# Gate and up rounds 3 to 10 as 2x2x2 block products in seven products

## The reference

```python
def swiglu(h, w_gate, w_up, w_down):
    return (jax.nn.silu(h @ w_gate) * (h @ w_up)) @ w_down
...
    h = h + swiglu(rms_norm(h, ffn_norm[i]), ffn_w_gate[i], ffn_w_up[i], ffn_w_down[i])
```

## Time and profile before

| what | value |
|---|---|
| median of 3 runs | 1115.61 us (1115.36 to 1115.8) |
| time of the profiled execution | 1115.62 us |
| its span | 1113.8 us |
| TensorE (PE) busy | 1102.3 us, 99% |
| VectorE (DVE) busy | 569.3 us, 51% |
| ScalarE (ACT) busy | 333.5 us, 30% |

### The profile page before, as it was taken

One profiled execution on the slowest core, in us unless ns is written; L12 is line 12 of the kernel. 1 busy time (PEld: TensorE's weight loads), 2 busy tenths in 40 slices (PEclk: granted clock), 3 DMA queues, 4 the chain that ended last, 5 costly groups with the idle time before them and its releaser, 6 DMA issues.

```text
span 1113.8 us, 13079 instructions
## 1 busy us (share of the span) xinstructions
PE 1102.3 (99%) x5056; PEld 916.9 (82%) x5056; DVE 569.3 (51%) x777; ACT 333.5 (30%) x407; POOL 40.1 (4%) x22
## 2 busy tenths in 40 slices
PE   8999999999999999999999999999999999999997
PEld 7888888888888888888888888888888888888886
DVE  6667766565454544333447545766454545433332
ACT  6667762322122121121232211323121221212221
POOL 0232230000000000000000000000000000000000
PEclk9999999999999999999999999999999999999999
DMA  7211221322322222222212233222323222222211
GB/s 275 95 66 48 75 74 40 114 113 76 113 82 107 80 108 104 75 104 104 104 75 78 111 114 107 83 79 109 114 75 113 81 108 81 107 104 98 76 63 75
DMA packets 16956, 106.08 MB, mean 95 GB/s; under 512 B 1888, under 2 KB 2144, under 8 KB 6432
## 3 DMA queue, kind: packets, MB, share of 16 engines
q1 hardware_dynamic: 16848, 105.43, 26.2%
q0 software_dynamic: 80, 0.26, 0.1%
HBM read 103.59 MB, written 2.10 MB: 95 GB/s over the span
## 4 chain that ended last, share of the span: by engine, by line
PE 97%; DMA 1%; DVE 1%; ACT 1%; SPq 0%; issue 0%; DVEq 0%; ACTq 0%
PE bank L406 32%; PE bank L408 32%; PE bank L407 32%; PE bank L560 1%; PE bank L546 1%; DMA head<-head_in 1%; PE bank L439 0%; DVE head L1405 0%; PE bank L548 0%; PE bank L445 0%; PE bank L453 0%; ACT a_hi L727 0%; ACT w_hi L713 0%; DVE mid_lo L1032 0%; ACT L849 0%
## 5 line engine op out<-in xcount | busy, mean ns | idle before, releaser
L406 PE MATMUL bank<-a_hi,w_hi 128*128 128x512 f32 x1000 | 391.9, 392 | 2.3 <-DVE a_lo L1078 2.0
L408 PE MATMUL bank<-a_hi,w_lo 128*128 128x512 f32 x1000 | 389.3, 389 | 0.0
L407 PE MATMUL bank<-a_lo,w_hi 128*128 128x512 f32 x1000 | 389.2, 389 | 0.0
L713 ACT ACTIVATE w_hi<-raw 128x2048 fp32r<-128x2048 f32 (+1 forms) x98 | 180.1, 1838 | 651.5 <-PE bank L408 651.3
L989 DVE TENSOR_TENSOR w_lo<-raw,w_hi 128x2048 fp32r<-128x2048 f32 (+1 forms) x90 | 200.1, 2223 | 131.5 <-ACT w_hi L713 131.5
L406 PEld LDWEIGHTS bank<-a_hi,w_hi 128*128 128x128 f32 x1000 | 187.7, 188 | 44.0 <-issue 4.2
L408 PEld LDWEIGHTS bank<-a_hi,w_lo 128*128 128x128 f32 x1000 | 187.7, 188 | 39.3
L407 PEld LDWEIGHTS bank<-a_lo,w_hi 128*128 128x128 f32 x1000 | 187.7, 188 | 39.0 <-issue 0.7
L406 PE MATMUL bank<-mid_hi,w_hi 128*128 128x512 f32 x496 | 194.0, 391 | 0.1
L408 PE MATMUL bank<-mid_hi,w_lo 128*128 128x512 f32 x496 | 193.1, 389 | 0.0
L407 PE MATMUL bank<-mid_lo,w_hi 128*128 128x512 f32 x496 | 193.0, 389 | 0.0
(11 more groups left out here) (140 smaller groups left out, 591.4 us busy)
## 6 DMA issues: line engine op xcount, KB each, us to landing
raw<-weights_in SPq DMA_DIRECT2D x82, 1024.0 KB, 4.8
raw<-weights_in SPq DMA_DIRECT2D x12, 768.0 KB, 4.2
raw<-weights_in SPq DMA_DIRECT2D x6, 512.0 KB, 3.7
work<-x SPq DMA_DIRECT2D x4, 512.0 KB, 6.1
head<-head_in SPq DMA_DIRECT2D x3, 512.0 KB, 8.3
out<-head SPq DMA_DIRECT2D x3, 512.0 KB, 3.4
out<-head SPq DMA_DIRECT2D x2, 256.0 KB, 4.0
head<-head_in SPq DMA_DIRECT2D x1, 293.5 KB, 3.3
```

What stands on the lines that cost most here:

```text
L406: pe.matmul(o, lhs[0], rhs[0], start=start, stop=False, skip_group_check=True)
L407: pe.matmul(o, lhs[0], rhs[1], start=False, stop=False, skip_group_check=True)
L408: return pe.matmul(o, lhs[1], rhs[0], start=False, stop=stop, skip_group_check=True)
L713: act.activation(w_hi[s][:, 0:n], raw[s][:, 0:n], ACT.Copy).then_inc(hi_split[s], 1)
```

## The change

Rounds 0 to 2 of each mixer (`PLAIN_ROUNDS`) stay full products, unrolled. In rounds 3 to 10 a pair of k tiles and the two output tiles form a 2x2 block matrix of the weights, and the pair of k tiles with the two halves of the tokens a 2x2 block matrix of the input (`HT` = 256 tokens). Winograd's form of Strassen's scheme multiplies these in seven block products instead of eight. The scheme needs sums of blocks:

- Weights, for each chunk: four sums on DVE (`forms`), three into `sums` (in `work`) and one in place in `raw[s]`; ACT makes high parts of `raw[s]` (2048 columns) and `sums` (1536); DVE makes both rests (`forms_split`). Blocks lie in another order in the stream.
- Input, once per mixer: in plain rounds 0 and 1 DVE makes four times (`x_forms`, one per pair of k tiles) the normed input with `rstd` and its sums, seven forms of 256 columns; ACT makes their high parts, DVE their rests (`x_forms_split`).
- Products: `winograd` on PE, 7 products x 4 pairs x 3 matmuls of 256 columns, into four banks (gate 0 to 3, up 4 to 7). Product 6, 3 and 7 add to a bank that ACT has copied in between (`copy`, `copy_last`).
- Results: DVE assembles the four quarter outputs from banks and copies (`top_left`, `top_right`, `bottom`), for gate into `work`, for up into `inner`; silu and the product with gate follow. The input forms carry `rstd`, so rounds 3 to 10 have no `scaled` and no product with it.
- The inner tiles stay whole in `inner` during the rounds. Their high parts (`inner_his`, ACT) and rests (`inner_rests`, DVE) are made in the last round and during down's first chunks.
- SBUF is laid out by stage in one arena, since the forms take the place of other tiles; the mixer's input is now `f_hi`, `f_lo`, the convolution's output tiles `u_hi`, `u_lo`. Down uses banks 0 to 3, the last transposes and sums swap banks 0 to 3 with 4 to 7. `clear_acc` moves from the first round to behind the last, as `acc` holds copies. Small vectors share one tensor, and the DMA scratch is 8192 bytes.

The core of the diff, its added lines (the silu, `scaled` and split lines that they replace are those of `ffn_round`, `silus` and `ffn` in the kernel before):

```diff
+PLAIN_ROUNDS = 3
+K_PAIRS = KD // 2
+HT = SEQ // 2
+BLOCK = K_PAIRS * P
+X_B11, X_B21, X_B22, X_T1, X_T2, X_T3, X_T4, X_FORMS = range(8)
+X_PAIR = X_FORMS * HT
...
+            def winograd(s, b0):
+                p, q, r, t = b0, b0 + 1, b0 + 2, b0 + 3
+                def block_product(b, weights, block, form, start):
+                    for k in range(K_PAIRS):
+                        c, n = block * BLOCK + k * P, k * X_PAIR + form * HT
+                        mm = product(bank[b][:, 0:HT], tuple(w[:, c:c + P] for w in weights),
+                                     tuple(x[:, n:n + HT] for x in X), start and k == 0, k == K_PAIRS - 1)
+                    return mm
+                blocks, block_sums = (w_hi[s], w_lo[s]), (s_hi[s], s_lo[s])
+                pe.wait_ge(w_split[s], T.add(f"slot{s}"))
+                for b in range(b0, b0 + 4):
+                    open_bank(b)
+                block_product(p, blocks, 1, X_B11, True).then_inc(product_done[1], 1)
+                pe.wait_ge(sums_split[s], T.add(f"sums{s}"))
+                block_product(q, block_sums, 0, X_T1, True).then_inc(product_done[5], 1)
+                block_product(r, blocks, 2, X_B21, True).then_inc(product_done[2], 1)
+                pe.wait_ge(product_copied, T.add("copied"))
+                block_product(p, block_sums, 1, X_T2, False).then_inc(product_done[6], 1)
+                pe.wait_ge(product_copied, T.add("copied"))
+                block_product(q, block_sums, 2, X_B22, False).then_inc(product_done[3], 1)
+                block_product(t, blocks, 3, X_T4, True)
+                pe.wait_ge(product_copied, T.add("copied"))
+                block_product(p, blocks, 0, X_T3, False).then_inc(chunk_done[s], 1)
             def ffn(made):
+                for f in range(PLAIN_ROUNDS):
+                    chunk(0, [0, 1], FFN_IN, ready=None if f else made)
+                    if f == 0:
+                        stat(4, KD)
+                    chunk(1, [2, 3], FFN_IN)
                 made += KD
+                pe.wait_ge(x_split, T.add("x", K_PAIRS))
+                with T.loop(pe, KF // 2 - PLAIN_ROUNDS, slot0=1, slot1=1, sums0=1, sums1=1, copied=6,
+                            b0=1, b1=1, b2=1, b3=1, b4=1, b5=1, b6=1, b7=1):
+                    winograd(0, 0)
+                    winograd(1, 4)
...
+            def blocks_hi(s):
+                k = T.add(f"slot{s}")
+                act.wait_ge(formed[s], T.add(f"formed{s}"))
+                act.wait_ge(chunk_done[s], k - 1)
+                act.activation(w_hi[s][:, :], raw[s][:, :], ACT.Copy).then_inc(hi_split[s], 1)
+            def sums_hi_of(s):
+                act.activation(s_hi[s][:, :], sums, ACT.Copy).then_inc(sums_hi[s], 1)
+            def copy(g, n):
+                b = 4 * g + (n == 5)
+                act.wait_ge(product_done[n], T.add(f"p{n}"))
+                act.activation(copies[g][(1, 5, 6).index(n)], bank[b][:, 0:HT], ACT.Copy).then_inc(product_copied, 1)
+            def copy_last(g):
+                act.wait_ge(drained[4 * g + 2], T.add(f"b{4 * g + 2}"))
+                act.wait_ge(chunk_done[g], T.now(f"slot{g}"))
+                act.activation(copies[g][0], bank[4 * g][:, 0:HT], ACT.Copy).then_inc(drained[4 * g], 1)
+                T.add(f"b{4 * g}")
+            def inner_his(ms, ready):
+                for m in ms:
+                    if m >= 2 * PLAIN_ROUNDS:
+                        act.wait_ge(inner_ready, ready + m + 1)
+                    take(tile(inner_hi, m), tile(inner, m))
+            def gate():
+                blocks_hi(1)
+                copy(0, 1)
+                sums_hi_of(1)
+                copy(0, 5)
+                copy(0, 6)
+                copy_last(0)
+            def ffn(layer):
+                for f in range(PLAIN_ROUNDS):
+                    if f < PLAIN_ROUNDS - 1:
+                        split(0)
+                    else:
+                        blocks_hi(0)
+                        sums_hi_of(0)
+                    if f == 0:
+                        rms(4, D)
+                    act.wait_ge(drained[1], T.add("b1"))
+                    for m in range(2):
+                        act.activation(tile(work, 3 + m), tile(work, 3 + m), ACT.Silu).then_inc(silu_done, 1)
+                    if f < PLAIN_ROUNDS - 1:
+                        x_hi_of(2 * f)
+                        split(1)
+                        x_hi_of(2 * f + 1)
+                banks_used(dict(b0=PLAIN_ROUNDS, b2=PLAIN_ROUNDS, b3=PLAIN_ROUNDS, b4=1))
+                rest = KF // 2 - PLAIN_ROUNDS
+                with T.loop(act, rest - 1, slot0=1, slot1=1, formed0=1, formed1=1, p1=2, p5=2, p6=2, b0=1, b1=1, b2=1, b3=1, b4=1, b6=1):
+                    gate()
+                    blocks_hi(0)
+                    copy(1, 1)
+                    sums_hi_of(0)
+                    copy(1, 5)
+                    silu(0, 1)
+                    silu(1, 3)
+                    copy(1, 6)
+                    copy_last(1)
+                gate()
                 split(0)
+                copy(1, 1)
+                copy(1, 5)
+                silu(0, 1)
+                silu(1, 3)
+                ready = layer * (KF - 2 * PLAIN_ROUNDS) - 2 * PLAIN_ROUNDS
+                inner_his(range(2), ready)
+                copy(1, 6)
+                inner_his(range(2, 6), ready)
+                copy_last(1)
+                inner_his(range(6, 12), ready)
                 split(1)
+                inner_his(range(12, KF), ready)
...
+            def forms(s):
+                blocks = [raw[s][:, k * BLOCK:(k + 1) * BLOCK] for k in range(4)]
+                s1, s2, s4 = (sums[:, k * BLOCK:(k + 1) * BLOCK] for k in range(3))
+                a21, a11, a12, a22 = blocks
+                v.wait_ge(raw_loaded[s], T.now(f"slot{s}") * 16)
+                wait(v, sums_split[1 - s], T.now(f"sums{1 - s}"))
+                do(v.tensor_tensor(s1, a21, a22, ALU.add))
+                settle()
+                do(v.tensor_tensor(s2, s1, a11, ALU.subtract))
+                do(v.tensor_tensor(a21, a11, a21, ALU.subtract))
+                settle()
+                v.tensor_tensor(s4, a12, s2, ALU.subtract).then_inc(formed[s], 1)
+            def forms_split(s):
+                v.wait_ge(hi_split[s], T.add(f"slot{s}") - 1)
+                v.tensor_tensor(w_lo[s][:, :], raw[s][:, :], w_hi[s][:, :], ALU.subtract).then_inc(w_split[s], 1)
+                v.wait_ge(sums_hi[s], T.add(f"sums{s}"))
+                v.tensor_tensor(s_lo[s][:, :], sums, s_hi[s][:, :], ALU.subtract).then_inc(sums_split[s], 1)
+            def x_forms(name, k):
+                buf = x_form[k % 2]
+                def form(n):
+                    return buf[:, n * HT:(n + 1) * HT]
+                b11, b21, b22, t1, t2, t3, t4, b12 = (form(n) for n in range(X_FORMS + 1))
+                halves = buf[:, :].rearrange("p (n c) -> p n c", c=HT)[:, 0:X_FORMS + 1:X_FORMS, :]
+                if k > 1:
+                    v.wait_ge(x_split, T.now("x") - 1)
+                do(v.scalar_tensor_tensor(halves, tile(xT, 2 * k).rearrange("p (n c) -> p n c", c=HT), gain(name, 2 * k),
+                                          rstd[:, :].rearrange("p (n c) -> p n c", c=HT), ALU.mult, ALU.mult))
+                do(v.scalar_tensor_tensor(buf[:, X_B21 * HT:(X_B22 + 1) * HT], tile(xT, 2 * k + 1), gain(name, 2 * k + 1),
+                                          rstd[:, :], ALU.mult, ALU.mult))
+                settle()
+                do(v.tensor_tensor(t1, b12, b11, ALU.subtract))
+                do(v.tensor_tensor(t3, b22, b12, ALU.subtract))
+                settle()
+                do(v.tensor_tensor(t2, b22, t1, ALU.subtract))
+                settle()
+                v.tensor_tensor(t4, b21, t2, ALU.subtract).then_inc(x_formed, 1)
+            def x_forms_split(k):
+                v.wait_ge(x_hi_made, T.add("x"))
+                cols = slice(k * X_PAIR, (k + 1) * X_PAIR)
+                v.tensor_tensor(x_lo[:, cols], x_form[k % 2][:, 0:X_PAIR], x_hi[:, cols], ALU.subtract).then_inc(x_split, 1)
+            def plain_round(f, name):
                 done(0)
                 all_ready()
+                if f == 0:
                     inverse_rms(4)
+                landed(2, 3)
+                scaled(3, 0)
+                scaled(4, 1)
+                if f < PLAIN_ROUNDS - 1:
+                    split(0)
+                    x_forms(name, 2 * f)
+                else:
+                    forms(0)
+                    forms_split(0)
                 for b in range(2):
                     v.wait_ge(silu_done, T.add("silu"))
+                    do(v.tensor_tensor(tile(work, 3 + b), tile(work, 3 + b), rstd[:, :], ALU.mult))
                 settle()
+                if f < PLAIN_ROUNDS - 1:
+                    x_forms_split(2 * f)
+                else:
+                    forms(1)
                 done(1)
                 for b in range(2):
```

(111 more changed lines are left out.)

126 lines of the change are left out of this document (69 added, 57 removed).

## The result

| | before | after |
|---|---|---|
| median of the runs | 1115.62 us (1115.36 to 1115.80) | 1122.05 us (1120.92 to 1122.78) |
| ratio, 95% interval | | 1.0057 (1.0040 to 1.0074) |
| profiled span | 1113.8 us | 1119.1 us |
| PE busy, matmuls | 1102.3 us, 5056 | 1096.3 us, 6208 |

The change makes the kernel 0.6% slower. Forecast was 0.3% faster. The time lies inside the range, on the other side of no change.

A forecast was written before the change was run, and what follows sets the result against it. PE, 99% busy, was taken as the bound. Arithmetic -26.7, stalls +19.5, a removed gap -0.3, clock +4.4 and restarts +0.3 sum to -2.8 us: 1112.8 us, range 1103 to 1124 (forecast's own 1107 to 1118).

The forecast's parts named there:

- the free parts: Outside the block rounds: moved inner operands, banks, buffers and weight block order were taken to cost nothing.
- the stall: Ahead of round 3, PE waits for bank drains queued behind DVE's forms: 10.4 and 9.0 us, 19.5 in all.
- rival 3: At block product boundaries: each of 224 costs 0.05 us, 11.2 us in all, giving 1124 us; chance 0.12.
- rival 4: Before and in the loop: DVE operations 10% longer make DVE the bound, +15.6 us, giving 1128; chance 0.08.
- The arithmetic: Rounds 3 to 10: 84 matmuls at 119.6 ns replace 48 at 226.7 per chunk; 32 chunks save 26.7 us.
- some 250 us: In block products: the loss if weight load and matmul ran in series, 213 ns; the prediction rejected it.
- The clock: After each stall before round 3, PE runs slower for some microseconds: 2.2 us each, +4.4 in all.
- rival 1: After the stalls before round 3: the clock does not fall, giving 1108.4 us; chance 0.15.
- The steady loop: Rounds 3 to 10 once running: DVE needs 18.0 us within PE's 20.1 us round, so added cost is 0.
- Rival 2: Before round 3: x forms are hidden and the loop starts on time, 1088.9 us; half a stall, 1101; chance 0.11.

The follow-up runs named there:

- experiment 1: The run `after_aligned`: the changed kernel with the arena 84 bytes shorter; 1110.14 us.
- after_aligned: The changed kernel with the arena 84 bytes shorter, so the weight slots and all behind them begin at a multiple of 64 bytes again; 1110.14 us, ratio 0.9948.
- experiment 2: The kernel before with only the weight buffers w_hi and w_lo moved 32 bytes; 1142.80 us, ratio 1.0241.
- experiment 3: The kernel before with the other operand's buffers (a, mid) moved 32 bytes, the weight buffers behind them 64; 1143.79 us, ratio 1.0249.
- experiment 4: The kernel before with both operands' buffers (a, mid, w) and everything behind them 32 bytes later; 1115.39 us, ratio 0.9999.
- experiment 5: The kernel before with w_hi, w_lo and what lies behind them 64 bytes later; 1142.89 us, ratio 1.0241.
- experiment 6: The kernel before with w_hi and w_lo 128 bytes later, by four small buffers declared ahead of them; 1140.08 us, ratio 1.0216.
- experiment 8: `after_aligned` with plain round 2's up chunk in banks 6 and 7, `forms(1)` before the silu products and ACT's copies earlier in the first block round; 1100.60 us.
- experiment 7: `after_aligned` with the rests of the input forms (x_lo) made by GpSimd instead of DVE; 1114.87 us, ratio 0.9991.

## Why the prediction was wrong

**The step that failed** is the last sentence on the free parts: "Banks, buffers and block order of weights move no instruction in time." I costed a new SBUF layout at nothing without a row that bounded it. It left `w` 96 bytes (modulo 512) from where the other operands stand, and 2952 matmuls of 512 columns went from 226.7 to 234.3 ns. That is 15.9 us in the stages around the rounds (table) and 576 x 7.6 ns = 4.4 us in the plain rounds, of which the stall gave 3.6 back (experiment 1). Without it the forecast's sign would have held: `after_aligned` is 5.7 us faster than before. The cause is shown by experiments 1 to 4. No rival named it either; rivals 3 and 4 led to "slower" by mechanisms of the loop, and none of that happened. So it is luck that the time lies inside the range: its upper end came from rival 3.

**The arithmetic** was right and 3 us too small: 29.9 us for 26.7. At agreeing offsets (`after_aligned`) the block products took 120.0 ns, the row's 119.6; the rest is the offset again, to the good. (The "some 250 us" for loads and matmuls in series is the loss against the forecast; against the kernel before, the same 213 ns give 2688 x 0.213 - 1536 x 0.2267 = 224 us. The earlier trace rows speak against both.)

**The stall** was the right mechanism at the right place, released by the drain that was named, and too large: 6.7 and 5.3 us for 10.4 and 9.0. Rows of DVE in after, which answer to the earlier trace rows: the reciprocal, two sums of which the second needs the first, and the drains.

```profile
224.31 3.36 DVE L1178 RECIPROCAL rstd<-bank 128x512 f32<-128x512 f32 x1 [8.06 <-ACT bank L798]
...
269.97 0.68 DVE L1440 TENSOR_TENSOR work<-raw 128x512 f32<-128x512 f32 x1
270.69 0.69 DVE L1442 TENSOR_TENSOR work<-work,raw 128x512 f32<-128x512 f32 x1
...
282.55 1.28 DVE L1508 TENSOR_TENSOR inner<-bank,work 128x512 f32<-128x512 f32 x2
```
From reciprocal to drained banks it is 59.5 us, not 61.45. A dependent operation starts 0.04 us after the end of the one before (270.65, 270.69), where I took 0.15 from a row with a CAST. Over the some twenty such starts in the queue that accounts for the 1.9 us. The other 1.8 us is PE, whose five chunks in that stretch are each 0.37 us longer. 10.4 - 1.9 - 1.8 = 6.7. In `after_aligned`, where the second term is gone, the stall is 8.5.

**The clock** fell, against rival 1. Windows of after, layer 0:

```profile
278.00:280.00 2.00, 0.00 (x0) 0.00 (x0) 1.97 (x4) 0.00 (x0) 0.00 (x0) 1.00 0.83 262
280.00:282.00 2.00, 0.00 (x0) 0.00 (x0) 1.93 (x4) 0.00 (x0) 0.00 (x0) 0.53 0.62 262
282.00:284.00 2.00, 0.02 (x1) 0.05 (x1) 1.83 (x3) 1.25 (x1) 0.00 (x0) 0.50 0.00 0
284.00:286.00 2.00, 2.00 (x9) 2.00 (x10) 1.31 (x1) 0.66 (x1) 0.00 (x0) 0.50 0.00 0
286.00:288.00 2.00, 2.00 (x16) 2.00 (x15) 0.98 (x1) 1.08 (x2) 0.00 (x0) 0.76 0.00 0
```
It falls from 2.4 to 1.2 GHz while PE is idle and comes back 3.0 us after PE works again (3.5 in layer 1); 12 intervals in layer 0 and 15 in layer 1 take 0.21 us in place of 0.12: 1.1 and 1.4 us. With the first matmul of each stall, 0.35 us to the next start (+0.5 for both, charged at 0.3), that is 3.0 us for 4.7. Taking the price from the kernel's start was sound in kind: there the starts are 0.21 us apart up to 5.54 and 0.11 from 5.71, as at half the clock, though the clock row reads full. The size is not a constant. In `after_aligned` the clock came back only 5.0 and 5.6 us after PE resumed, 22 and 24 intervals were slow, and the loss was 2.0 and 2.2 us, close to the 2.2 that I charged.

**The steady loop** cost nothing, as said: no PE wait, boundaries at 0.12 us (326.46 to 326.58), a DVE that waits for ACT's high part and for a copy (in after 1.05 us ahead of 337.54 and 0.67 ahead of 335.73). Rival 3's boundaries and rival 4's slower DVE operations are refuted; the one of 2048 columns takes 2.29 us as before. Rival 2, half a stall, is nearest to what was measured, but its time (1101) would have needed agreeing offsets as well. Down's first chunks have no gap.

The sum as it came out: -29.9 + 12.0 + 3.0 - 0.3 + 4.4 = -10.8 in the rounds (-10.6 in the table), + 15.9 around them = +5.1 of span; measured +5.3. (The medians differ by 6.4 us; the profiled execution of after was the fastest of its four.) For `after_aligned` the same sum is -25.6 (120.0 ns) + 15.6 + 4.8 - 0.3 = -5.5, measured -5.4 of span: with the layout put right, the prediction's mechanism holds, 2.7 us further down than forecast.

## What to carry to other kernels

A change of SBUF layout is part of the cost of a change: print the address of both operands of the matmuls before and after, and compare their difference modulo 512 bytes. If a stage that the change did not touch has another pace, look there before anything else. And read which bank the first product behind a boundary opens, and what is queued ahead of its drain: opening an empty bank, with two changes of order beside it, was worth 9.5 us here, while the one attempt to shorten the queue made it longer.

## What the runs showed of the hardware that was not expected

- The pace of back-to-back fp32r matmuls, each with its own weight load, depends on the difference of the two operands' byte offsets in SBUF. With a difference of 0 modulo 512: 226.7 ns for 512 columns and 119.6 to 120.0 for 256. With 32, 64, 96 or 128: 232.4 to 234.3 for 512 columns, and with these or 480 116.7 to 118.3 for 256, but for the values stage of after (96: 119.6). So each difference tried costs 2.5 to 3.4% at 512 columns, and most gain 1 to 3% at 256. 256 and most other differences were not tried, and which step inside TensorE makes it so is not shown. The Trainium skill (TensorE: Matmul & The Clock Gate, section "Step-by-step: what each phase is for") says that TensorE has two independent read ports for the two operands and that loading the next weights takes no read bandwidth from the running matmul. By that, the offset would be free; experiments 2, 3, 5 and 6 show 24 to 28 us for it, and the measurement decides.
- The clock can fall to 1.2 GHz when PE has already resumed: after a wait of 1.94 us at 818.82 it was half from 820 to 822 (experiment 8). Waits about as long in layer 0 of that run had no fall behind them.
- A DVE operation with both inputs in SBUF, issued while GpSimd runs one that reads SBUF, is held up until that one ends (experiment 7): one of 128x512 and 0.69 us took 4.59.
